# The order of the three passes in the pair of products that begins a stage

## What is computed

```python
h = _rmsnorm(x, p['norm_mix'][0]) * (1 + sc_m) + sh_m        # stage w1 begins: h @ a_w1
x = x + g_m * (silu(layernorm(conv(glu(h @ a_w1)))) @ a_w2)  # stage w2 begins at "@ a_w2"
h = _rmsnorm(x, p['norm_ffn'][0]) * (1 + sc_f) + sh_f        # stage ffn0: h @ f_wup[0], conv, gate, @ f_wdown[0]
hkv = _rmsnorm(x, p['norm_kv']) * (1 + sc) + sh              # stage kv: hkv @ w_kv
h = _rmsnorm(x, p['norm_mix'][1]) * (1 + sc_m) + sh_m        # stage q: h @ w_q, attention, @ w_o
h = _rmsnorm(x, p['norm_ffn'][1]) * (1 + sc_f) + sh_f        # stage ffn1
```

## Time and profile before

| | us |
|---|---|
| median of three runs | 2826.91 |
| the profiled execution, its own time | 2835.29 |
| its span, first to last instruction | 2833.5 |
| TensorE busy | 2558.2 (90%) |
| VectorE busy | 1309.0 (46%) |
| ScalarE busy | 975.4 (34%) |
| GpSimd busy | 937.5 (33%) |
| mean granted TensorE clock | 0.918 of full |

### The profile page before, as it was taken

How to read it: one execution, slowest core, us unless ns; L and a number is a source line. 1 busy time by engine, 2 the same in 40 slices (tenths; PEclk the granted TensorE clock), 3 DMA queues, 4 the chain that set the end, 5 groups by cost and what they waited for, 6 DMA issues and landing times.

```text
span 2833.5 us, 39892 instructions
## 1 busy us (share of the span) xinstructions
PE 2558.2 (90%) x15866; PEld 2419.7 (85%) x15866; DVE 1309.0 (46%) x1515; ACT 975.4 (34%) x2208; POOL 937.5 (33%) x489
## 2 busy tenths in 40 slices
PE   4899958799999999999698998947799999999995
PEld 2777738799999999999698996837799999999995
DVE  3677864444444444444711204586543333333335
ACT  3311214443333333333611303332533333333333
POOL 1322214244444444442341300034253343434340
PEclk6899968899999999999899956768899999999997
DMA  7476540033344444422022161210111111111101
GB/s 263 149 213 201 161 140 30 1 112 131 134 146 153 152 153 152 153 75 75 15 97 67 55 233 63 75 45 16 51 45 45 46 45 46 45 46 45 46 31 67
DMA packets 90311, 270.48 MB, mean 95 GB/s; under 512 B 27584, under 2 KB 37504, under 8 KB 88352
## 3 DMA queue, kind: packets, MB, share of 16 engines
q1 hardware_dynamic: 90144, 267.96, 27.7%
HBM read 236.12 MB, written 58.67 MB: 104 GB/s over the span
## 4 chain that ended last, share of the span: by engine, by line
PE 80%; DVE 6%; issue 4%; DMA 4%; SPq 2%; POOL 2%; ACT 2%; POOLq 0%; DVEq 0%; ACTq 0%
PE bank L263 47%; PE bank L1504 16%; PE bank L279 5%; PE bank L1654 1%; DMA w_raw<-in_ws 1%; SPq L645 1%; PE bank L1572 1%; PE bank L373 1%; PE bank L365 1%; PE bank L302 1%; PE bank L1598 1%; DMA w_raw<-in_att 1%; DMA out_cap<-full 1%; PE bank L1717 1%; PE bank L1613 1%
## 5 line engine op out<-in xcount | busy, mean ns | idle before, releaser
L263 PE MATMUL bank<-h_hi,w_hi 128*128 128x352 f32 x2832 | 617.6, 326 | 8.4 <-issue 7.6
L263 PE MATMUL bank<-h_hi,w_lo 128*128 128x352 f32 x2832 | 611.6, 323 | 0.0
L263 PE MATMUL bank<-h_lo,w_hi 128*128 128x352 f32 x2832 | 610.4, 324 | 0.0
L249 POOL TENSOR_TENSOR w_lo<-w_raw,w_hi 128x1024 fp32r<-128x1024 f32 x182 | 483.9, 2660 | 136.7 <-ACT w_hi L1048 123.3
L263 PEld LDWEIGHTS bank<-h_hi,w_hi 128*128 128x128 f32 x2832 | 481.4, 189 | 31.0 <-issue 24.6
L1151 DVE SCALAR_TENSOR_TENSOR cv<-u,cwb,cv 128x1072 f32<-128x1072 f32 x88 | 151.9, 1727 | 762.6 <-ACT cv L908 762.6
L263 PEld LDWEIGHTS bank<-h_hi,w_lo 128*128 128x128 f32 x2832 | 487.0, 188 | 0.0
L263 PEld LDWEIGHTS bank<-h_lo,w_hi 128*128 128x128 f32 x2832 | 481.6, 188 | 0.0
L245 POOL CAST w_hi<-w_raw 128x1024 fp32r<-128x1024 f32 x168 | 202.2, 1203 | 610.0 <-DMA w_raw<-in_ws 325.6
L468 ACT ACTIVATE tb<-bank,mod 128x352 f32<-128x352 f32 x552 | 261.1, 544 | 253.2 <-PE bank L1504 171.5
L779 POOL TENSOR_TENSOR z_lo<-cv,z_hi 128x1024 fp32r<-128x1024 f32 x44 | 110.4, 2508 | 476.1 <-ACT z_hi L926 476.1
(11 more groups left out here) (237 smaller groups left out, 2818.3 us busy)
## 6 DMA issues: line engine op xcount, KB each, us to landing
w_raw<-in_ws SPq DMA_DIRECT2D x182, 512.0 KB, 5.5
w_mod<-in_wm SPq DMA_DIRECT2D x72, 512.0 KB, 5.8
out_kvs<-in_cache SPq DMA_DIRECT2D x8, 4088.0 KB, 20.3
w_modf<-in_wm SPq DMA_DIRECT2D x40, 512.0 KB, 4.2
w_raw<-in_att SPq DMA_DIRECT2D x36, 512.0 KB, 3.2
shifts<-full SPq DMA_DIRECT2D x128, 129.5 KB, 2.5
x<-in_xt SPq DMA_DIRECT2D x8, 1056.0 KB, 10.4
out_kvs<-in_cache SPq DMA_DIRECT2D x8, 1016.0 KB, 9.1
```

The source lines that it names most:

```text
L249: e.tensor_tensor(w_lo[s][:, :], w_raw[s][:, :], w_hi[s][:, :].bitcast(F), ALU.subtract).then_inc(split[s], 1)
L263: mm = e.matmul(bank[3 * b + c][:, 0:CW], w[s][:, kk * P:(kk + 1) * P], a[:, kk, c * CW:(c + 1) * CW], start=(kk == 0 and q == 0), stop=(k ...
```

## The change

`product_pair` keeps its 144 matmuls and their operands. The loop over the two slots moves inside the loop over the three passes, and the order of the passes becomes w_hi·h_hi, w_lo·h_hi, w_hi·h_lo. The first pass of a block waits for `h_hi_done` (h_hi of this block written), and the third for `h_ready`, as the whole block did before. The signals `used[A0]` and `used[A1]` stand at the last matmul of each slot in the last block's third pass. Nothing else in the kernel is changed.

```diff
             for kk in range(KD):
-                e.wait_ge(h_ready[kk % 2], 4 * a_n + kk // 2 + 1)
-                for s in (A0, A1):
-                    for q, (w, a) in enumerate(((w_hi, h_hi), (w_hi, h_lo), (w_lo, h_hi))):
+                for q, (w, a) in enumerate(((w_hi, h_hi), (w_lo, h_hi), (w_hi, h_lo))):
+                    if q == 0:
+                        e.wait_ge(h_hi_done, 8 * a_n + kk + 1)
+                    elif q == 2:
+                        e.wait_ge(h_ready[kk % 2], 4 * a_n + kk // 2 + 1)
+                    for s in (A0, A1):
                         for c in range(NC):
                             mm = e.matmul(bank[3 * s + c][:, 0:CW], w[s][:, kk * P:(kk + 1) * P],
                                           a[:, kk, c * CW:(c + 1) * CW], start=(kk == 0 and q == 0),
                                           stop=(kk == KD - 1 and q == 2))
-                    if kk == KD - 1:
-                        mm.then_inc(used[s], 1)
+                        if kk == KD - 1 and q == 2:
+                            mm.then_inc(used[s], 1)
```

## The result

| | before | changed |
|---|---|---|
| median | 2834.53 us (20 runs, 2825.81 to 2846.27) | 2825.19 us (20 runs, 2808.60 to 2831.71) |
| ratio, 95% interval | | 0.9967 (0.9952 to 0.9982) |
| the profiled execution, its own time | 2835.29 us | 2830.36 us |

The changed kernel is 9.3 us faster, 0.33%, with an interval of 5 to 14 us. The forecast was 13.8 us, so the direction is right and the size too large, within the interval. The predicted time of 2813.1 us is 12.1 us off, and the range of 2808 to 2819 missed. Of these 12.1 us, 7.6 are the level: the three runs known of the kernel before (2826.9 us) lay at the fast end of what it does, and its twenty runs, with a median of 2834.5, spread over 20 us. The other 4.5 us are the gain.

A forecast was written before the change was run, and what follows sets the result against it. TensorE was taken to bound the kernel, idle at six stage heads behind GpSimd's h_lo. 18.8 us at the starts, less 4.85 at the pairs' ends and 0.2 for D0's weights, gave 13.8 us: 2813.1 us, range 2808 to 2819.

The forecast's parts named there:

- The start of a stage: First pass of each of six stages starts behind h_hi instead of h_lo: 18.8 us gained.
- The third pass meets h_lo in time: Block 0's h_lo arrives with 0.06 us to spare, k=4 in w1 with 0.2; stalls cost nothing, bound 3 us.
- The waits added: One more wait per block, 48 in all; already met when reached, so they cost nothing.
- The end of the pair: ScalarE empties A0's banks 0.97 us later in w2, ffn0, kv, q and ffn1: 4.85 us lost.
- The idle times given as a sign for the other stages: TensorE's idle time behind the pair should grow to 1.1 us (kv, q) and 1.4 us (ffn0, ffn1).
- The weights of D0: Behind ffn0's pair these weights don't move and become late: 0.2 us lost; in ffn1 ready 0.6 us ahead of need.
- The clock: Low clock at each pair's start moves forward, lasting as long; could add 2.8 us or take 2 us.
- Carried to the end undiminished: Behind each pair the chain stays on TensorE or on what waits for it, so all 13.8 us reach the end.
- the one that nothing is lost at the end: Rival: ScalarE's late start at the pair's end is covered; gain 18.8 us, 2808.1 us; chance 0.04.
- the one that the change does nothing: Rival: TensorE still can't start before h_lo, only losses up to 4.85 us stay, 2831.8 us; chance 0.04.
- the gain is carried only in part: Rival: transfers behind w1 and q take up 3.5 and 1.5 us; 8.8 us stay, 2818.1 us; chance 0.10.
- The clock that holds a whole pair back: Rival: pauses at third passes keep whole pairs at 1.2 GHz, 17 us a stage, slower; chance 0.02.

The follow-up runs named there:

- third trace: The changed kernel, no edit, run a third time against the kernel before: ratio 0.9948, 2820.47 us.
- Late wait: The changed kernel, but each block's first pass waits for h_ready, the new order kept; against the kernel before, ratio 1.0012.
- its second one: The kernel before, unchanged, run again for a second trace: ratio 0.9992.
- both: Changed kernel with last block slot by slot, h_ready awaited ahead of it, and D0, D1 fetched before SyncE's wait for VectorE; against the kernel before 0.9955, 2824.50 us.
- best: both, plus GpSimd waiting in ffn0, kv, q, ffn1 for the last h_lo before splitting weights; against the kernel before 0.9937, 2815.55 us; again 0.9933, 2816.98 us.

## Why the prediction was right and wrong

**The level.** The step that failed was the one from the profiled execution to the median: "the same difference on it gives 2826.91 - 13.8 = 2813.1 us". I saw that they differed by 8.4 us and treated the difference as constant. The profiled execution, 2835.29 us, was typical of the kernel, and the three runs of 2826.4 to 2827.6 us were not: twenty runs have a median of 2834.53. 2835.29 - 13.8 = 2821.5 us, which I had worked out, would have been 3.7 us off. The range had no term for the spread between executions. Of the 12.1 us by which the forecast missed, 7.6 are this step (2834.5 - 2826.9) and 4.5 the gain (13.8 - 9.3).

**The gain.** Three comparisons give 0.9967, 0.9962 and 0.9948, in the mean 0.9959 or 11.6 us; the heads give 12.0 us. That the first comparison gave only 9.3 lies within its interval of 5 to 14. The forecast of 13.8 us is right in its mechanism and 1.8 us too large: the pair got 1.4 us longer, where the sum had nothing, and its end lost 5.6 us, where the sum had 5.05; the start gave 0.1 us more. Step by step:

- *The start of a stage*, 18.8 us: right. TensorE's idle time before the pairs fell from 50.8 to 31.8 us, 19.0 us.
- *The third pass meets h_lo in time*, nothing: right for block 0, where 0.06 us of margin held in each stage. Later blocks cost 0.7, 1.1 and 1.1 us in the three traces, by the distance of the starts. This is the larger part of the 1.4 us, and within the bound of 3 us. In w1, ffn0 and kv it was the third pass of k=4, for which the prediction found 0.2 us left at a low clock of 4.5 us: where the low clock lasted only 2.9 to 3.3 us, TensorE caught up with GpSimd and waited 0.3 us; w1 of the third trace, with 4.1 us, didn't wait. I had walked through w1 and taken the producers to be the same elsewhere; in kv VectorE's last h_lo takes 3.34 us, which the trace of before shows and I didn't read.
- *The waits added*, nothing: nothing is seen of them.
- *The end of the pair*, 4.85 us: right. Late wait shows 4.9 us, and w2's next product went from 0.59 to 1.56 us behind ScalarE, 0.97 us. The idle times given as a sign for the other stages were misread, though: before it was 0.12 us in ffn0 and nothing in kv, so that 0.97 more makes 1.09 and not 1.4, and 0.93 to 0.99 in kv and q and not 1.1.
- *The weights of D0*, 0.2 us in ffn0 and none in ffn1: the wrong way round. In ffn0 the first product behind the pair waited for ScalarE, 1.09 and 1.10 us, in two traces, and for these weights, 1.13 us, in the third. In ffn1 I had GpSimd 0.6 us ahead of need and took its time from the trace of before. In that trace, its second one and late wait GpSimd begins to split D0 22.7 us behind the first h_hi; in the three traces of the changed kernel 24.1 to 24.2 us. The step that failed is that these weights "don't move". SyncE's issue of `hist` took 1.44 us instead of 0.43 in the first trace, and that of D0 itself 1.09 and 1.19 instead of 0.43 in the two others, each beside an instruction load. It cost 0.6 to 0.8 us in the head of ffn1, and in one trace of three 1.5 us more behind it, through the clock.
- *The clock* moved forward with the start, as assumed, by about the same length: over the six heads it was low for 27.2 and 25.7 us before, and for 28.2, 27.0 and 25.6 in the three traces of the changed kernel. The means differ by 0.5 us, 0.2 us of work.
- *Carried to the end undiminished*: not contradicted. The time gained as much as the heads, 11.6 and 12.0 us. It isn't shown more closely than that: the sections between the heads differ by up to 7 us from trace to trace in w1, 6 in ffn0 and 16 in the attention, and those of w1 differ by 4 us between two traces of the same kernel before.

Of the rivals, the one that nothing is lost at the end is refuted by the waits behind ScalarE, and the one that the change does nothing by the chain. That the gain is carried only in part isn't refuted to better than these spreads. The clock that holds a whole pair back did not come; the low clock came behind an idle stretch at the pair's end in one trace, at 1.5 us.

The Trainium skill says, on the page "TensorE: Matmul & The Clock Gate" in Part 1, that the number of slow matmuls at a start changes from run to run. The traces agree: the same code in ffn0 was at the low clock for 3.2 us in one trace of the changed kernel and for 6.1 in another.

## What to carry to other kernels

When a consumer is let start earlier, look at both ends: what it signals last, and what it then meets sooner than it was ever ready. Here 18.9 us gained at the starts left 12: 4.9 went because the last signal had moved by six matmuls, 0.7 because the next weights had only been on time for the old schedule, and some 1.4 inside the pair, mostly because the consumer caught up with its producers. Two helpers that share the last step should be put in order by hand, since the one that is in no hurry can slow down the one that is waited for. And a wait of one's own belongs where the data is first read: six matmuls too early, it was most of the 6.9 us of pauses in both. A predicted time needs the spread of the executions: one profile and three runs that differ by 8 us are a warning, not a constant.

## What the runs showed of the hardware

VectorE's subtraction of 128x1056 takes 1.26 us alone and 3.3 us where GpSimd splits a weight unit at the same time; a wait of GpSimd's for the subtraction's end brings it back to 1.26 us in ffn0, kv, q and ffn1.

Whether the clock falls behind a short pause is not decided by its length alone. Behind the pair of ffn1 it fell behind 1.90 us of idle time and not behind 1.74 and 1.69 us, which a length alone could explain. But at the first border of ffn0's loop it fell behind 1.15 us in the first trace of the changed kernel, and not behind 1.69 us in the second trace of best (us, TensorE's busy time and matmuls, granted clock, DMA share, GB/s):

```profile
748.90:752.30 3.40, 3.40 (x13) 0.50 0.00 0
```

```profile
745.00:752.00 7.00, 6.99 (x43) 1.00 0.02 5
```
